# Softmax attentions of two transformer blocks: order of the inverses in memory, and new lists for three engines

## What is computed

```python
def chunk_causal_softmax_attention(q, k, v):          # mla: 8 heads of 96 / 64
        z = jnp.einsum("bhqd,bshd->bhqs", q_blk, k).astype(jnp.float32) * scale
        p = jax.nn.softmax(jnp.where(allowed, z, -jnp.inf), axis=-1)
        return jnp.einsum("bhqs,bshd->bhqd", p.astype(v.dtype), v)
...
        y_mla = jnp.einsum("bsc,cd->bsd", o_mla * jax.nn.silu(gate_mla), w_o_mla[l])

def fox_attention(h, w_in, b_f, w_out):               # fox: 16 heads of 64
        s = jnp.einsum('bhqd,bhkd->bhqk', qb, k, preferred_element_type=jnp.float32)
        s = s + cb[..., :, None] - c[..., None, :]
        s = jnp.where(k_pos[None, :] <= q_pos[:, None], s, NEG_INF)
        pr = jax.nn.softmax(s, axis=-1)
        return jnp.einsum('bhqk,bhkd->bhqd', pr.astype(v.dtype), v)
```

## Time and profile before

| | us |
|---|---|
| median of 3 runs | 1709.67 |
| lowest and highest run | 1707.98 and 1710.61 |
| the profiled execution | 1708.22 |
| its span, first to last instruction | 1706.3 |
| PE busy in the span | 1676.5 (98%) |
| DVE busy | 1285.8 (75%) |
| ACT busy | 952.9 (56%) |
| multiplications of line 3087 | 12, at 329.2 to 680.6 |
| writes of inverses, line 2211 | 24, issue to landing 1.4 to 6.1 |
| read-backs, line 2219 | 24, issue to landing 2.7 to 6.0 |

### The profile page before, as it was taken

One profiled execution on the slowest core, in us unless ns is written; L12 is line 12 of the kernel. 1 busy time (PEld: TensorE's weight loads), 2 busy tenths in 40 slices (PEclk: granted clock), 3 DMA queues, 4 the chain that ended last, 5 costly groups with the idle time before them and its releaser, 6 DMA issues.

```text
span 1706.3 us, 25098 instructions
## 1 busy us (share of the span) xinstructions
PE 1676.5 (98%) x9279; PEld 1441.0 (84%) x9279; DVE 1285.8 (75%) x2054; ACT 952.9 (56%) x1717; POOL 169.7 (10%) x147
## 2 busy tenths in 40 slices
PE   9999999999999998999999999999999999999998
PEld 7888877878788886789899998878887999999977
DVE  6378877776567887688798986785566979898966
ACT  4267875655436765477546364652235866464655
POOL 2011212000300000220000002420003000000041
PEclk9999999999999999999999999999999999999998
DMA  8222124224243333243233443313322432323621
GB/s 274 81 73 75 40 74 101 84 66 148 75 112 85 87 91 93 75 173 124 75 123 99 124 164 120 109 55 109 111 87 93 156 122 100 99 100 99 236 74 50
DMA packets 158163, 180.72 MB, mean 106 GB/s; under 512 B 22121, under 2 KB 130182, under 8 KB 156262
## 3 DMA queue, kind: packets, MB, share of 16 engines
q1 hardware_dynamic: 150790, 159.22, 30.1%
q10 hardware_dynamic: 7264, 20.05, 3.3%
HBM read 161.96 MB, written 12.63 MB: 102 GB/s over the span
## 4 chain that ended last, share of the span: by engine, by line
PE 82%; DVE 10%; ACT 3%; DMA 2%; issue 2%; POOL 1%; ACTq 0%; DVEq 0%; POOLq 0%; SPq 0%
PE bank L1171 24%; PE bank L1172 24%; PE bank L1173 24%; DMA raw_weights<-in_w_mlp_down 2%; DVE split_weights L2704 2%; PE bank L1520 2%; PE bank L1544 1%; PE bank L1439 1%; POOL ssum L3666 1%; DVE act_b L2704 1%; DVE split_weights L2656 1%; PE bank L1428 1%; DVE work L3087 1%; DVE act_a L2706 1%; PE bank L1557 1%
## 5 line engine op out<-in xcount | busy, mean ns | idle before, releaser
L1171 PE MATMUL bank<-act_a,split_weights 128*128 128x512 f32 (+1 forms) x1360 | 526.0, 387 | 7.5 <-DVE act_a L2704 3.7
L1173 PE MATMUL bank<-act_a,split_weights 128*128 128x512 f32 (+1 forms) x1360 | 519.0, 382 | 0.0
L1172 PE MATMUL bank<-act_a,split_weights 128*128 128x512 f32 (+1 forms) x1360 | 518.6, 381 | 0.0
L1171 PEld LDWEIGHTS bank<-act_a,split_weights 128*128 128x128 f32 x1360 | 256.2, 188 | 60.2 <-issue 6.1
L1173 PEld LDWEIGHTS bank<-act_a,split_weights 128*128 128x128 f32 x1360 | 255.9, 188 | 50.5
L1172 PEld LDWEIGHTS bank<-act_a,split_weights 128*128 128x128 f32 x1360 | 256.3, 188 | 45.2 <-issue 0.2
L1171 PE MATMUL bank<-act_b,split_weights 128*128 128x256 f32 (+1 forms) x648 | 207.3, 320 | 1.2 <-DVE split_weights L3398 1.2
L1173 PE MATMUL bank<-act_b,split_weights 128*128 128x256 f32 (+1 forms) x648 | 206.4, 319 | 0.0
L1172 PE MATMUL bank<-act_b,split_weights 128*128 128x256 f32 (+1 forms) x648 | 206.3, 318 | 0.0
L2646 DVE TENSOR_TENSOR split_weights<-raw_weights,split_weights 128x2048 fp32r<-128x2048 f32 x55 | 127.8, 2323 | 75.2 <-ACT split_weights L1882 62.4
L1882 ACT ACTIVATE split_weights<-raw_weights 128x2048 fp32r<-128x2048 f32 x51 | 97.3, 1908 | 118.4 <-PE bank L1173 118.4
(11 more groups left out here) (357 smaller groups left out, 3221.8 us busy)
## 6 DMA issues: line engine op xcount, KB each, us to landing
raw_weights<-in_w_mlp_up SPq DMA_DIRECT2D x32, 1024.0 KB, 5.3
raw_weights<-in_w_mlp_down SPq DMA_DIRECT2D x32, 1024.0 KB, 5.3
raw_weights<-in_w_in SPq DMA_DIRECT2D x18, 1024.0 KB, 5.2
raw_weights<-in_w_conv_in SPq DMA_DIRECT2D x12, 1024.0 KB, 5.2
raw_weights<-in_w_attn_in SPq DMA_DIRECT2D x16, 512.0 KB, 5.2
raw_weights<-in_w_ple_gate SPq DMA_DIRECT2D x8, 1024.0 KB, 5.1
raw_weights<-in_w_out SPq DMA_DIRECT2D x4, 1024.0 KB, 5.4
raw_weights<-in_w_attn_in SPq DMA_DIRECT2D x4, 1024.0 KB, 5.3
```

Source lines behind the costliest of these rows:

```text
L1171: nc.tensor.matmul(dst, w[0], a[0], start=first, stop=False)
L1172: nc.tensor.matmul(dst, w[0], a[1], start=False, stop=False)
L1173: mm = nc.tensor.matmul(dst, w[1], a[0], start=False, stop=last)
```

## The change

1. The inverses are written in order of tokens, one element of 4 bytes at a time, and the multiplication reads them in one run of 512. Each of a pair's two heads has its own semaphore for the write.
2. The step `f` goes. The second half's read-back (b1) stands at the end of the same pair's list on ACT.
3. On DVE `k0` stands earlier in each list. Maxima, exponentials, high and low parts change places in all lists of ACT and DVE. Output tile 2 of fox is split at the end of pair 6 instead of at the start of pair 7. The lists of the last pair are new. PE's lists stay as they are.

```diff
-        inverse_out = sem("inverse_out")
+        inverse_out = [sem(f"inverse_out_{hh}") for hh in range(2)]
...
-        ACT_MLA = "e0 e1 y1 p0 e2 p1 f1 w0 e3 p2 p3 s2 w1 d0 e4 e5 p4 y2 e6 b0 p5 e7 p6 r0 p7 s3 d1 r1"
-        DVE_MLA = "m0 m1 m2 m3 p0 p1 p2 m4 p3 n0 m5 c0 c1 c2 y1 m6 p4 k0 c3 m7 p5 s2 p6 n1 g0 p7 y2 x0 x1 s3 g1"
+        ACT_MLA = "e0 e1 y1 p0 e2 p1 w0 e3 p2 p3 s2 w1 d0 e4 e5 p4 y2 e6 p5 e7 b0 p6 r0 p7 d1 s3 r1 b1"
+        DVE_MLA = "m0 m1 m2 m3 p0 p1 k0 p2 m4 p3 n0 m5 c0 c1 c2 y1 m6 p4 m7 c3 p5 s2 n1 p6 g0 p7 y2 x0 x1 s3 g1"
         PE_FOX = "z0 g0 z1 g1 z2 t0 t1 z3 g2 z4 t2 g3 z5 t3 g4 z6 t4 t5 z7 v0 g5 t6 t7 g6 g7 v1"
-        ACT_FOX = "w0 y0 e0 e1 w1 p0 e2 f1 s2 p1 e3 p2 p3 e4 e5 d0 y1 e6 s3 p4 p5 b0 e7 r0 p6 p7 d1 r1"
-        DVE_FOX = "m0 m1 c0 m2 c1 p0 m3 s2 p1 m4 m5 p2 p3 n0 y0 m6 k0 c2 m7 c3 y1 p4 p5 g0 n1 p6 p7 x0 x1 s3 g1"
+        ACT_FOX = "w0 y0 e0 e1 w1 p0 e2 s2 p1 e3 p2 p3 e4 e5 y1 d0 p4 e6 p5 e7 s3 r0 d1 p6 b0 p7 r1 b1"
+        DVE_FOX = "m0 m1 c0 m2 c1 p0 m3 s2 p1 m4 k0 m5 p2 p3 n0 y0 m6 p4 c2 m7 p5 c3 y1 n1 g0 p6 p7 x0 x1 s3 g1"
...
-        ACT_NEAR = "y0 e0 e1 p0 p1 f1 e2 w0 w1 e3 p2 p3 e4 d0 e5 e6 o0 o1 p4 p5 b0 y1 r0 e7 p6 p7 s2 d1 r1"
-        DVE_NEAR = "m0 m1 m2 m3 p0 y0 c0 c1 p1 p2 m4 m5 p3 n0 m6 k0 c2 c3 o0 o1 p4 y1 m7 p5 g0 x0 x1 n1 p6 p7 s2"
+        ACT_NEAR = "y0 e0 e1 p0 p1 e2 w0 w1 e3 p2 p3 e4 e5 e6 d0 o0 o1 p4 p5 y1 r0 e7 o2 b0 p6 p7 d1 s2 r1 b1"
+        DVE_NEAR = "m0 m1 m2 k0 m3 p0 y0 c0 c1 p1 p2 m4 m5 p3 n0 m6 c2 c3 o0 o1 p4 y1 m7 p5 g0 x0 x1 n1 p6 p7 s2 o2"
...
         PE_LAST = "z0 z1 z2 g1 t0 z3 t1 g2 t2 t3 z4 z5 z6 g3 t4 z7 g4 v0 t5 g5 t6 t7 g6 v1"
-        ACT_LAST = "e0 s1 p0 e1 f1 y0 e2 o2 e3 p1 o3 w0 p2 y1 o4 p3 e4 o5 d0 w1 e5 o6 e6 e7 b0 p4 p5 d1 r0 p6 p7 b1 r1"
-        DVE_LAST = "m0 m1 m2 h1 p0 m3 s1 o2 y0 p1 o3 c0 p2 m4 o4 k0 y1 p3 n0 o5 m5 c1 m6 m7 c2 n1 c3 p4 p5 o6 g0 p6 p7 g1"
...
+        ACT_LAST = "e0 e1 s1 p0 e2 p1 e3 p2 o3 p3 e4 y0 o4 p4 e5 w0 e6 o5 d0 e7 p5 d1 y1 r0 o6 p6 p7 b0 w1 b1 r1"
+        DVE_LAST = "m0 m1 m2 h1 s1 m3 p0 p1 m4 o3 m5 p2 p3 o4 m6 n0 y0 p4 k0 m7 o5 p5 n1 c0 o6 y1 g0 c1 p6 p7 c2 c3 g1"
...
-                    nc.scalar.dma_start(inverse_rows[hh, :].rearrange("(p j) -> p j", p=P), pair_sums(i, hh))\
-                        .then_inc(inverse_out, 16)
+                    nc.scalar.dma_start(inverse_rows[hh, :].rearrange("(j p) -> p j", p=P), pair_sums(i, hh),
+                                        allow_slow_non_contiguous=True)\
+                        .then_inc(inverse_out[hh], 16)
...
-                    act.wait_ge(inverse_out, 16 * (h + 1))
+                    act.wait_ge(inverse_out[hh], 16 * (h // 2 + 1))
...
-                    by_tiles = out_.rearrange("p (j q) -> p j q", j=TT)
-                    V.tensor_tensor(by_tiles, by_tiles, sq[:, 0, :].rearrange("p (q j) -> p j q", j=TT), ALU.mult)\
+                    V.tensor_tensor(out_, out_, sq[:, 0, :], ALU.mult)\
```

More of the change, by code:

```diff
@@ L473, in hybrid_block_kernel @@
         PE_LAST = "z0 z1 z2 g1 t0 z3 t1 g2 t2 t3 z4 z5 z6 g3 t4 z7 g4 v0 t5 g5 t6 t7 g6 v1"
-        ACT_LAST = "e0 s1 p0 e1 f1 y0 e2 o2 e3 p1 o3 w0 p2 y1 o4 p3 e4 o5 d0 w1 e5 o6 e6 e7 b0 p4 p5 d1 r0 p6 p7 b1 r1"
-        DVE_LAST = "m0 m1 m2 h1 p0 m3 s1 o2 y0 p1 o3 c0 p2 m4 o4 k0 y1 p3 n0 o5 m5 c1 m6 m7 c2 n1 c3 p4 p5 o6 g0 p6 p7 g1"
-        ACT_MLA_LAST = "e0 e1 y1 p0 e2 p1 f1 w0 e3 p2 p3 w1 d0 e4 e5 p4 o0 e6 b0 p5 o1 e7 p6 r0 d1 p7 o2 b1 r1"
-        DVE_MLA_LAST = "m0 m1 m2 m3 p0 p1 p2 m4 p3 n0 m5 c0 c1 c2 y1 m6 p4 k0 c3 m7 p5 o0 n1 p6 g0 o1 p7 x0 x1 o2 g1"
+        ACT_LAST = "e0 e1 s1 p0 e2 p1 e3 p2 o3 p3 e4 y0 o4 p4 e5 w0 e6 o5 d0 e7 p5 d1 y1 r0 o6 p6 p7 b0 w1 b1 r1"
@@ L479, in hybrid_block_kernel @@
+        DVE_LAST = "m0 m1 m2 h1 s1 m3 p0 p1 m4 o3 m5 p2 p3 o4 m6 n0 y0 p4 k0 m7 o5 p5 n1 c0 o6 y1 g0 c1 p6 p7 c2 c3 g1"
+        ACT_MLA_LAST = "e0 e1 y1 p0 e2 p1 w0 e3 p2 p3 w1 d0 e4 e5 p4 o0 e6 p5 e7 o1 b0 p6 r0 p7 d1 o2 r1 b1"
+        DVE_MLA_LAST = "m0 m1 m2 m3 p0 p1 k0 p2 m4 p3 n0 m5 c0 c1 c2 y1 m6 p4 m7 c3 p5 o0 n1 p6 g0 o1 p7 x0 x1 o2 g1"
         EARLY_OUT = {"mla": 3, "fox": 7}
@@ L2248, in pair_of_heads @@
                             inverse_to_half(pair, s)
-                        elif what == "f":
-                            if pair:
-                                inverse_to_half(pair - 1, s)
                         elif what == "e":
```

## The result

The changed kernel takes **1815.16 us** (median of 4 runs, 1811.29 to 1823.02) against 1709.65 us for the kernel before on the same chip: ratio 1.0627 (95% interval 1.0607 to 1.0646). It is 105.5 us slower; the forecast was 1707.4, with 1714 as its upper end. The profiled execution has a span of 1811.5 us, against 1706.3.

The account below looks back on a forecast made before the run. TensorE was taken to bound the kernel (82% of the chain), so only its waits count. Terms -3.6 - 2.4 - 0.5 - 4.2 + 8.4 = -2.3 us on the profiled 1708.22 us gave a median of 1707.4 us, range 1699 to 1714.

Parts of the forecast that it names:

- The write's price: Write of the inverses in 4-byte pieces: lands 0.6 us later, at most 4.2 us later.
- Rival B: Fox: element-wise write is slow; from 1.0 us extra the kernel is slower, with 2.2 us more 1720 us; chance 0.2.
- Rival A: Fox: the write's packets interleave with the weight loads', so the read-back loss vanishes: -10.7 us, 1699; chance 0.14.
- Who waits for it: Fox pairs 0 to 4 and near-last pair: ACT waits at b1, holding PE 0.4 to 2.4 us; mla nothing.
- The Trainium skill: Write of the inverses: one descriptor per element, rearrange it; by its count 3.6 us more loss in each of six places.
- mla, -3.6: mla: moving k0 ahead of p2 ends PE's hold before t7, 1.2 us in each of 3 pairs.
- fox, -2.4: Fox: moving k0 between m4 and m5 ends PE's hold before t6, 0.49 us in each of 5 pairs.
- p4 and p5 more: Fox lists: p4 and p5 now precede splitting c3; with multiplication 1.07 less, loads go out 0.4 us earlier.
- The read-back b1, +8.4: Fox: b1 at the list's end waits for its write and delays PE in six pairs; loss 8.4 us, 6.0 to 10.8.
- Pair 6, -0.5: Near-last fox pair: e5 moves ahead of the wait for d0, so t5 is no longer held 0.51 us.
- The last pair, -4.2: Last fox pair: no wait at g2 and an earlier last tile gain 4.2 us, despite small new waits.
- rival C: Last pair gives nothing, through new waits on o6 and p7 or k0 not fitting: +4 us, 1711; chance 0.1.

Follow-up runs that it names:

- hidden_write: Kernel before with 4-byte write, one-run multiplication and both read-backs in the next pair (except each attention's last): 1779.09 us; control with 16-byte write and old multiplication 1709.92.
- mla_only: Kernel before with only the mla stage's new ACT and DVE lists, old write and multiplication: 1704.32 us, ratio 0.9977.
- all_p4_f1_back: fox_p4_back with the last pair's p4 also later, fox's second-half read-back in the next pair, and pair 6's k0 in its old place: 1701.72 us.
- fox_p4_back: lists_16b with p4 and p5 in the fox lists behind e6 and m7 again: 1702.02 us, ratio 0.9967.
- lists_16b: Changed kernel's lists with the old 16-byte write and multiplication; a pair's first write also waits for both earlier read-backs: 1711.58 us, ratio 1.0016.

## Why the prediction was wrong, step by step

- **The write's price** is the step that failed. The working put the new write's landing at 0.6 us more, four times the burst of the earlier trace rows, and its upper bound at 4.2 us, four times the whole landing. It measures 7.5 to 8 us more on a quiet chip (8.9 and 9.4 against 1.4), and up to 10 beside the stores. The burst grew less than said, from 0.2 to 0.4 us and not to 0.8; but a landing is the sending and what follows it, and nearly all of the cost is behind the last packet: 8.1 us there instead of 0.4. No row of before showed that part for small pieces. The bound from above took it to grow fourfold at most. Nor does a piece of 4 bytes cost at most what one of 16 does: 128 of them side by side land in 7.4 us, 128 of 16 bytes in 1.4. Rival B named the mechanism and the point from which it decides (1 us); its size, 2.2 us more, was far too small as well. Rival A, that the write's packets mix with the loads', didn't come: before, d1 is issued at 548.46 and its packets start at 551.5, when those of the loads thin out, and with the 16-byte write in the new lists d1 of a fox pair lands after 3.3 to 6.4 us.
- **Who waits for it.** The sum let ACT wait at b1 in six places. With a landing of 9 to 14 us b0 is caught as well, in mla too: 23 places.
- **What runs beside.** No step had the write slow other DMAs. hidden_write costs 69 us over its control, 28.0 of them PE's waits for a copy that has nothing to do with the write.
- **The Trainium skill** ("DMA: Bandwidth & Descriptors", Rules for kernel authors) pointed the right way: it warns of one descriptor for each element. By its count the loss was to grow by 3.6 us in each place; the measurement decides, with some 8 us, and with the finding that the count alone isn't it, since the same 512 pieces 64 bytes apart land in 1.8 us.
- **mla, -3.6**: right, -3.6 to -3.9, with the old multiplication. The hold was m7's wait for k0, and its new place removes it: mla_only has no idle row of PE before t7.
- **fox, -2.4**: right in size, -2.4 in all_p4_f1_back; but not with the lists of the change. The step "p4 and p5 more" priced their move at their own duration and overlooked that p4 waits for v0. That is 8.5 us.
- **The read-back b1, +8.4**: far too much for the old write. It is 1.3 us (fox_p4_back against all_p4_f1_back, start of fox to pair 6), and nothing in lists_16b. In lists_16b ACT comes to b1 so late, 4.9 us behind d1, that the write (3.7) has landed. In fox_p4_back's pair 1, d1 goes out 4.4 us behind d0 and its write lands 10.0 us behind d0, where the sum had 11.1 (0.6 of it the surcharge for 4-byte pieces). Holds of 0.4 to 2.4 us in six pairs shrink to one of about 1 us, in the pair whose write takes 6.4. The landing behind the loads (4.1 to 6.4 us) and the restart 0.5 us later are as the sum had them.
- **Pair 6, -0.5**: right, -0.7. **The last pair, -4.2**: wrong, at most -0.9 with the lists of the change, and what was gained at g2 is lost at p4 and o5, with half the clock behind it. This is rival C in what it gave, though by other waits than those on o6 and p7.
- With the old write and multiplication the kernel takes 1711.6 us: within the range, but by luck, because two errors of 8 us nearly cancel.

## What to carry to other kernels

Price a DMA whose pieces are 4 or 8 bytes by its landing, measured on its own, not by its bytes, packets or burst; and before you let it run in the background, look at the landing of what runs beside it. If you move a step up in an engine's list, read what it waits for, most of all the last reader of the buffer that it writes: whatever stands behind it in the list waits too.
